# GpSimd's modulation multiplies as two-tensor operations over a broadcast column

## The reference

```python
s_lat = jax.nn.silu(c)
for layer in range(DEPTH):
    shift, scale, gate = jnp.split(s_lat @ w_mod[layer] + b_mod[layer], 3, axis=-1)
    x_in = x * (1.0 + scale[:, None, :]) + shift[:, None, :]
...
c_act = jax.nn.silu(c)
for l in range(DEPTH):
    shift, scale, gate = jnp.split(c_act @ w_ada[l] + b_ada[l], 3, axis=-1)
    h = rms_norm(x, norm_w[l]) * (1.0 + scale[:, None, :]) + shift[:, None, :]
    y = jnp.concatenate([o_gla, o_gdn, o_diff], axis=-1) @ w_out[l]
    x = x + gate[:, None, :] * y
```

## Time and profile before

| | us |
|---|---|
| median of 3 runs | 2849.5 |
| lowest and highest | 2842.16, 2854.03 |
| the profiled execution | 2847.17 |
| its span, first to last instruction | 2845.4 |
| PE busy in it | 2700.5 (95%) |
| DVE busy | 1663.4 (58%) |
| ACT busy | 1208.8 (42%) |
| POOL busy | 1644.8 (58%) |

### The profile page before, as it was taken

How to read it: one execution, slowest core, us unless ns; L and a number is a source line. 1 busy time by engine, 2 the same in 40 slices (tenths; PEclk the granted TensorE clock), 3 DMA queues, 4 the chain that set the end, 5 groups by cost and what they waited for, 6 DMA issues and landing times.

```text
span 2845.4 us, 50999 instructions
## 1 busy us (share of the span) xinstructions
PE 2700.5 (95%) x22151; PEld 2497.1 (88%) x22151; DVE 1663.4 (58%) x1905; ACT 1208.8 (42%) x1438; POOL 1644.8 (58%) x875
## 2 busy tenths in 40 slices
PE   5799999999999999999999969999999899999999
PEld 2489988888888999989989959999899899998899
DVE  2343444554454657686676655764775557646763
ACT  1243433333433334344576345633453446334442
POOL 0057777997777799988555703064668430546510
PEclk9699999999999999999999979999999999999999
DMA  9998998998887997776555836755667666555665
GB/s 338 288 316 262 269 265 253 277 292 252 237 239 233 281 264 225 222 209 199 156 149 165 229 97 167 186 149 155 184 166 218 177 167 174 157 153 164 168 171 153
DMA packets 891422, 599.19 MB, mean 211 GB/s; under 512 B 22070, under 2 KB 830400, under 8 KB 890688
## 3 DMA queue, kind: packets, MB, share of 16 engines
q1 hardware_dynamic: 887376, 582.83, 72.3%
q10 hardware_dynamic: 3824, 13.11, 1.2%
HBM read 589.46 MB, written 6.29 MB: 209 GB/s over the span
## 4 chain that ended last, share of the span: by engine, by line
PE 77%; DVE 8%; DMA 6%; POOL 5%; ACT 2%; SPq 1%; issue 1%; DVEq 0%; POOLq 0%; ACTq 0%
PE G L2393 57%; DMA ring<-in_w_mod_dram 3%; POOL ring L825 3%; PE A L2332 2%; DMA const<-in_w_mod_dram 2%; DVE ring_r L1465 2%; POOL mod_rows L833 1%; PE A L2453 1%; PE A L2459 1%; PE A L2456 1%; PE G L2475 1%; POOL ring L832 1%; PE A L2638 1%; PE A L2494 1%; DMA ring<-in_w_ada_dram 1%
## 5 line engine op out<-in xcount | busy, mean ns | idle before, releaser
L2393 PE MATMUL G<-H_r,ring_r 128*128 128x256 f32 x10032 | 1695.4, 286 | 37.0 <-DVE S_r L1454 18.7
L825 POOL TENSOR_SCALAR ring<-ring,act_in 128x512 f32<-128x512 f32 x448 | 947.2, 2125 | 1047.5 <-DMA ring<-in_w_ada_dram 820.9
L2393 PEld LDWEIGHTS G<-H_r,ring_r 128*128 128x128 f32 x10032 | 1469.2, 191 | 69.5 <-issue 50.2
L1465 DVE TENSOR_TENSOR ring_r<-ring,ring_r 128x2048 fp32r<-128x2048 f32 x346 | 839.3, 2427 | 278.4 <-ACT ring_r L866 277.4
L866 ACT ACTIVATE ring_r<-ring 128x2048 fp32r<-128x2048 f32 x346 | 661.7, 1912 | 328.3 <-DMA ring<-in_a_w_out_dram 88.3
L2393 PE MATMUL G<-M_r,ring_r 128*128 128x256 f32 x4528 | 787.7, 283 | 0.0
L2393 PEld LDWEIGHTS G<-M_r,ring_r 128*128 128x128 f32 x4528 | 643.7, 189 | 9.2 <-issue 8.6
L2393 PE MATMUL G<-S_r,ring_r 128*128 128x256 f32 x1920 | 546.3, 285 | 0.0
L2393 PEld LDWEIGHTS G<-S_r,ring_r 128*128 128x128 f32 x1920 | 369.1, 192 | 3.4 <-issue 3.3
L833 POOL TENSOR_TENSOR mod_rows<-mod_rows,ring 128x512 f32<-128x512 f32 x196 | 331.8, 1693 | 15.4
L832 POOL TENSOR_TENSOR ring<-ring 128x512 f32<-128x512 f32 x196 | 320.1, 1633 | 16.3
(11 more groups left out here) (440 smaller groups left out, 2547.2 us busy)
## 6 DMA issues: line engine op xcount, KB each, us to landing
ring<-in_w_in_dram SPq DMA_DIRECT2D x120, 1024.0 KB, 5.7
ring<-in_a_w_in_dram SPq DMA_DIRECT2D x98, 1024.0 KB, 6.9
ring<-in_w_ada_dram SPq DMA_DIRECT2D x192, 512.0 KB, 6.6
const<-in_w_mod_dram SPq DMA_DIRECT2D x192, 256.0 KB, 5.4
ring<-in_c_w_in_dram SPq DMA_DIRECT2D x48, 1024.0 KB, 5.9
ring<-in_w_mod_dram SPq DMA_DIRECT2D x16, 2048.0 KB, 18.3
ring<-in_a_w_out_dram SPq DMA_DIRECT2D x32, 1024.0 KB, 6.5
ring<-in_w_out_dram SPq DMA_DIRECT2D x32, 1024.0 KB, 5.9
```

Source lines behind the costliest of these rows:

```text
L825: g.mark(pool.tensor_scalar(w[:, i, :], w[:, i, :], act_in[:, k, c:c + 1], None, ALU.mult))
L1465: v.tensor_tensor(w_low(tl), w_raw(tl), w_up(tl).bitcast(F32), ALU.subtract).then_inc(w_lo, 1)
L2393: ins = pe.matmul(G[tl.bank][:, 0:SEQ], w, x, start=(k == 0 and n_ == 0), stop=(k == KT - 1 and n_ == 2))
```

## The change

One call is replaced: the multiply of a piece by a per-row scalar becomes a multiply of two tensors, the second being the same one-column operand read again for each of the 512 columns. The result is written over the piece as before. The number of instructions, their order, the waits and counts, the transfers and the buffers stay as they are; on PE, DVE, ACT and SP nothing differs.

```diff
                     for i in range(2):
                         k = 2 * u + i
-                        g.mark(pool.tensor_scalar(w[:, i, :], w[:, i, :], act_in[:, k, c:c + 1], None, ALU.mult))
+                        g.mark(pool.tensor_tensor(w[:, i, :], w[:, i, :], act_in[:, k, c:c + 1].broadcast_to((P, 2 * BW)), ALU.mult))
                     g.settle()
```

## The result

The changed kernel takes 2867.5 us (median of 5 runs, 2861.7 to 2878.6) against 2848.1 us for the kernel before (5 runs, 2842.2 to 2854.0). The ratio is 1.0074, with a 95% interval of 1.0052 to 1.0096: it is slower by 0.7%, 19 us, where 2839 us was forecast. A repeat on another chip gave 1.0079 (1.0056 to 1.0102).

A forecast was written before the change was run, and what follows sets the result against it. PE was taken as the bound, busy 2700.5 of 2845.4 us, with some idle time due to POOL. Gains of 5.0 + 0.6 + 2.5 + 1.5 + 1.0 = 10.6 us took the median of 2849.5 to 2839 us, range 2828 to 2853.

The forecast's parts named there:

- The cost of the edit itself: On POOL: the new multiply takes 1.27 us instead of 1557 ns, and POOL's busy time falls by 190 us.
- D: 1204 to 1241 us, DVE and POOL taking turns: shorter multiplies shorten DVE's turns; 1.5 us gained, ends 0 and 6.7.
- A: 495 to 625 us: SP's wait for POOL halves and PE waits less for weights; 5.0 us gained, ends 0 and 7.4.
- B: 1000 to 1035 us: PE's waits for DVE shrink as loads behind POOL's come earlier; 0.6 us, ends 0 and 2.3.
- C: 1094 to 1167 us: PE's 2.53 us wait for POOL's finished sum goes whole; 2.5 us gained, ends 1 and 3.
- E: From 1250 us on: POOL is in DVE's way by tenths, meetings dealt anew; 1.0 us gained, ends -3 and 5.
- The one on the slow side: Rival: the broadcast multiply takes 2188 ns instead of 1557, making POOL the bound; about 40 us lost, 2890 us, chance 0.09.

The follow-up runs named there:

- the 320-column kernel: The kernel before with its scalar multiply over 320 of the 512 columns: 2825.6 us, ratio 0.9941.
- the mixed kernel: The kernel before with the broadcast multiply for the first 9 of the 28 pairs of blocks, scalar for the rest: 2835.0 us, ratio 0.9970; repeated, 0.9972.
- the late half of the change: The kernel before with the scalar multiply for the first 9 pairs of blocks and the broadcast multiply for the other 19: ratio 1.0106.

## Why the prediction was wrong

**The cost of the edit itself: the size was off, to the good side.** I took 1.27 us, with 1.26 as the lower end. It is 1.03, below the range. The nearest row, the add, reads two different tensors. So a minimum of another instruction of the same form was no lower bound. The mean came out at 1515 ns where 1.7 us was forecast, and POOL's busy time fell by 257 us, not 190.

**The step that failed** is in the same part: "As the stretch is about the same for the one-input and the two-input form, I let it stay." That sentence is about how long DVE stretches POOL. How long POOL stretches DVE I priced only in D, and there by the multiply's length and not by its form; everywhere else the edit counted as one on POOL alone. Nor did the stretch stay: it is 1515 / 1030 = 1.47. The equal mean stretch (1.36 against 1.34) hid two different things. The rows had a sign of it, unread: the multiply's longest duration is 5602 ns against 3390 and 3432 of the adds. An add was at worst held up by one DVE operation of 2.2 us; a multiply now and then by more than one, since it let one after the other pass. The longest duration alone is a weak sign, for the new multiply has one of 4817 ns and in the second profile one of 5098. The count says more: over 2.25 us above their least were 23 and 24 of the 448 multiplies in the two profiles of before, 3 and 3 in those of after, and none of the 392 adds of before. And in the earlier trace rows the slowed DVE operation at 1225.00, 2.32 us instead of 1.22, is one that stands beside an add, at 1224.08. With 0.27 us for each of the 448 multiplies (119 us of DVE between the 320-column kernel and after) the sum would have had a term that it lacked altogether. What this term costs the kernel the runs show too: two kernels with nearly equally quick multiplies (1.09 and 1.03 us) are at 0.9941 and 1.0079, 39 us apart.

**A** was right in the mechanism: SP's wait for POOL halved (26.8 to 12.4 us), PE's wait fell from 6.1 to 3.2 and in the second profile to 3.8, and tiles 0 to 98 gained about 6 us, where 5.0 were forecast. That gain is little more than the 4 to 5 us by which two profiles of one kernel differ there, but the mixed kernel, with 0.9970 and 0.9972, bears it out as a time.

**B and C** turned over. The wait for POOL's sum is gone in both profiles of after, as C said. But "next late is DVE's work on X, a few tenths" was off by a factor of ten: waits of 3.5 and 5.3 us at L1684 stand there, 2.8 and 5.6 in the second profile. Tiles 98 to 138 lost 8 to 10 us instead of gaining the 3.1 us of B and C.

**D** was read as a place where DVE stands behind a multiply and gains 0.3 us at each turn. The multiply did slow DVE there before, but little: four scalar operations of L1671 took 2.29 us instead of 1.39. Now three such groups take 4.07, 3.85 and 4.74 us beside a multiply and the adds behind it. The single ones have a median of 1068 ns instead of 664:

```profile
L1671 DVE TENSOR_SCALAR M<-X,mod x16: 400/664/772, 1209.3 to 1237.3; 128x256 f32<-128x256 f32 x16
```
```profile
L1671 DVE TENSOR_SCALAR M<-X,mod x16: 400/1068/1448, 1212.0 to 1240.3; 128x256 f32<-128x256 f32 x16
```

(The line's own view, first before, then after; duration ns min/median/max.) DVE's round, from one L1668 to the next, grew from 9.0 to between 9.2 and 9.5 us, where D needed it to shrink. POOL did run dry in between, as D's upper end has it, with waits of 1.1 to 5.1 us for its loads, and that didn't help DVE.

**E** was given +1.0 with ends at -3 and 5, "dealt anew". It was no deal: tiles 138 to 254 lost 13 to 23 us, while the 320-column kernel, whose POOL is as quick, gained 5 to 6 there. Which of DVE's waits on PE's path make up the loss is not shown.

**The rivals.** The one on the slow side had the right sign by the wrong mechanism: it needed a multiply over 1557 ns. The Trainium skill's page "GPSIMD Engine Reference", section 4.1 "Engine selection", from which I took it, has two-input operations as the dear ones on GpSimd; here the order is the other way round, 1030 ns for the two-input multiply against 1557. The page that did bear on the case is another one of the Trainium skill, "SBUF — State Buffer", section "Who interferes with whom": VectorE and GpSimd share a port pair, and a VectorE operation with two SBUF inputs contends with a GpSimd one that reads SBUF. The runs agree (18.4 and 19.7 us against 13.3 for two-input operations on GpSimd, 14.6 for the one-input one, which reads SBUF as well). What that sentence of the Trainium skill doesn't say is that the price goes by the form of the GpSimd operation: with one tensor input it is GpSimd that pays most of it.

**What POOL's speed is worth** was forecast at 10.6 us and measured, without the two-input form, at 17 us (0.0059 of 2843.8, the 320-column kernel), with an interval of 10 to 23. With it went 22 to 32 us less on DVE (1631.8 against 1663.4 and 1653.7), which the forecast hadn't counted. So the gain side was about right or too small, not too large. The net of 19 to 23 us is a gain of some 17 us and a loss of about 39, of which the sum had only the first.

That the late half of the change costs 1.06% and the whole one 0.79% is explained by the gain in the first half. What stays open is how the 39 us divide among L1684, L2168 and the others: it can't be read from two profiles that differ by 17 us from each other.

## What to carry to other kernels

When GpSimd and VectorE work side by side, cost an edit on one for what it does to the other: compare not only an operation's mean but how often its duration exceeds its own length by more than one VectorE operation, which shows whether it gives way or takes turns. And look at the other engine's busy time, which moved here by 87 us without an edit to it. A GpSimd operation that gets shorter can lose time if VectorE is nearer to the critical path and the new form keeps it out. In this kernel the faster form paid in the first part (up to about tile 79 of 346, 0.3%) and the yielding form behind it. Short pieces of the holding form took the loss away for the multiplies, but gained nothing for the adds.

## What the runs showed of the hardware

- GpSimd, 128 x 512 f32: multiply by a column scalar 1557 ns, by the same column as a broadcast second tensor 1030 ns, by itself 1032 ns, addition or multiplication by another tensor 1262 ns. For 256 columns the addition took 715 to 721 ns at the least.
- A two-input operation on GpSimd held each of six subtracts of 2048 columns on VectorE for 0.84 us (operation of 1.03 us) or 1.06 us (of 1.26), and was itself held up to 2.05 us at a meeting. A one-input one held every second subtract, for 0.41 us, and grew from 1.56 to as much as 4.84 us.
- VectorE's one-input multiply of 2048 columns was held as well (1.21 or 1.62 us beside the one-input form, 2.06 and 2.28 beside the two-input ones), and so were subtracts of 256 columns (0.41 us free, 1.25 and 1.48 us beside the two-input ones).
- In the kernel before, POOL's 392 adds cost 117 us more of VectorE's time and 25 us more of the kernel's (0.95%) than one-input operations of about their length.
